# Decoder trunk, feed-forward: the last pair of chunks takes column blocks 2 and 3 by seven products instead of eight

## The reference

```python
def conv_glu_ffn(x, w_in, conv_w, conv_b, w_out):
    h = x @ w_in                                  # 2048 -> 2 x 5632
    hc = conv_b + sum(hp[:, k:k + S] * conv_w[k] for k in range(3))
    gate, val = jnp.split(hc, 2, axis=-1)
    return (gelu(gate) * val) @ w_out             # 5632 -> 2048

x = layer_norm(alpha * x + conv_glu_ffn(x, ...), gain, bias)
```

## Time and profile before

| | |
|---|---|
| median of three runs | 2014.38 us |
| the profiled execution | 2014.52 us |
| its span, first to last instruction | 2012.7 us |
| TensorE busy | 2003.1 us (100%), 10708 matmuls |
| weight loads busy | 1715.5 us (85%) |
| VectorE busy | 1657.6 us (82%), 1529 instructions |
| ScalarE busy | 1221.7 us (61%) |
| HBM read | 386.36 MB, 193 GB/s |

### The profile page before, as it was taken

The page is one execution under the profiler, slowest core; times in us unless marked ns, Lnnn a source line. Parts: engine busy times, 40 slices in busy tenths (PEclk is TensorE's granted clock), DMA queues, the critical chain, the costliest instruction groups (busy, mean ns, idle before and its releaser), DMA issues.

```text
span 2012.7 us, 25848 instructions
## 1 busy us (share of the span) xinstructions
PE 2003.1 (100%) x10708; PEld 1715.5 (85%) x10708; DVE 1657.6 (82%) x1529; ACT 1221.7 (61%) x1439; POOL 5.8 (0%) x10
## 2 busy tenths in 40 slices
PE   9999999999999999999999999999999999999998
PEld 8888888888888888888888877888888888888886
DVE  5446566769899998999997786776989899898998
ACT  5443444767566675766744664476766667576672
POOL 0000000000000000000000000000000000000001
PEclk9999999999999999999999999999999999999999
DMA  9554464655656565556656345465565656655662
GB/s 331 196 189 151 162 232 166 204 190 194 212 183 204 194 208 197 193 197 208 219 204 196 126 133 188 161 209 188 197 213 176 209 193 205 203 192 194 207 225 109
DMA packets 194824, 390.40 MB, mean 194 GB/s; under 512 B 6969, under 2 KB 9747, under 8 KB 193683
## 3 DMA queue, kind: packets, MB, share of 16 engines
q1 hardware_dynamic: 194419, 388.49, 57.6%
q10 hardware_dynamic: 288, 0.26, 0.1%
HBM read 386.36 MB, written 2.10 MB: 193 GB/s over the span
## 4 chain that ended last, share of the span: by engine, by line
PE 98%; DVE 1%; DMA 0%; SPq 0%; issue 0%; ACT 0%; DVEq 0%
PE ps L1550 37%; PE ps L1560 19%; PE ps L1879 6%; PE ps L1881 6%; PE ps L1880 6%; PE ps L1577 6%; PE ps L1579 5%; PE ps L1578 5%; PE ps L1700 1%; PE ps L2029 1%; PE ps L2004 1%; PE ps L2012 1%; PE ps L1667 0%; PE ps L1705 0%; PE ps L1538 0%; PE ps L1817 0%
## 5 line engine op out<-in xcount | busy, mean ns | idle before, releaser
L925 DVE TENSOR_TENSOR w_lo<-raw,w_hi 128x2048 fp32r<-128x2048 f32 x352 | 796.8, 2282 | 75.2 <-ACT w_hi L566 74.8
L566 ACT ACTIVATE w_hi<-raw 128x2048 fp32r<-128x2048 f32 x352 | 664.3, 1909 | 284.1 <-DMA raw<-ffn_w_in 116.6
L1550 PE MATMUL ps<-T,w_hi 128*128 128x512 f32 x3264 | 764.6, 390 | 0.0
L1550 PEld LDWEIGHTS ps<-T,w_hi 128*128 128x128 f32 x3264 | 605.7, 188 | 122.9 <-issue 1.7
L1560 PEld LDWEIGHTS ps<-T,w_lo 128*128 128x128 f32 x3264 | 405.8, 191 | 10.0 <-issue 2.0
L1560 PE MATMUL ps<-T,w_lo 128*128 128x256 f32 x3264 | 410.6, 283 | 0.0
L1879 PE MATMUL ps<-w_hi,forms 128*128 128x512 f32 x464 | 180.5, 389 | 0.0
L1881 PE MATMUL ps<-w_hi,forms 128*128 128x512 f32 x464 | 180.5, 389 | 0.0
L1577 PE MATMUL ps<-w_hi,T 128*128 128x512 f32 (+1 forms) x448 | 177.4, 396 | 0.1
L1579 PE MATMUL ps<-w_hi,T 128*128 128x512 f32 (+1 forms) x448 | 173.9, 388 | 0.0
L1578 PE MATMUL ps<-w_lo,T 128*128 128x512 f32 (+1 forms) x448 | 173.6, 388 | 0.0
(11 more groups left out here) (188 smaller groups left out, 1849.7 us busy)
## 6 DMA issues: line engine op xcount, KB each, us to landing
raw<-ffn_w_in SPq DMA_DIRECT2D x176, 1024.0 KB, 5.1
raw<-ffn_w_out SPq DMA_DIRECT2D x88, 1024.0 KB, 5.1
raw<-even_w_in SPq DMA_DIRECT2D x38, 1024.0 KB, 5.1
raw<-attn_w_qkv SPq DMA_DIRECT2D x20, 1024.0 KB, 5.2
raw<-even_w_out SPq DMA_DIRECT2D x16, 1024.0 KB, 5.1
raw<-attn_w_out SPq DMA_DIRECT2D x16, 1024.0 KB, 5.2
arena<-ln_gain SPq DMA_DIRECT2D x4, 1024.0 KB, 4.9
arena<-ln_bias SPq DMA_DIRECT2D x4, 1024.0 KB, 7.4
```

Source lines behind the costliest of these rows:

```text
L566: nc.scalar.activation(w_hi[:, s % RING], raw_at(s), ACT.Copy).then_inc(hi_ready, 1)
L925: vec.tensor_tensor(lo_at(s), raw_at(s), w_hi[:, s % RING].bitcast(F32), ALU.subtract).then_inc(lo_ready, 1)
L1550: ins = mm(ps[:, banks[j]], w_hi[:, s % RING, k, P * j:P * j + P], T[:, GK * kg + k], start=kg == 0 and k == 0, stop=kg == KG - 1 and k == ...
```

## The change

C of the last pair becomes a quad like the others, in both layers. On TensorE seven products of 12 matmuls stand where four blocks of 24 stood. The form X_21 is not made any more. VectorE makes four sums, seven low parts and nine takes for C where it made four low parts and two adds. The sums of this one quad (`LATE`) don't lie in `lnp`, since the gain and bias are loaded there by then, but in the second half of T (`late_sums`, with their low parts `late_lo` at the same place). Three of them are made in the middle of Q (`between`), the fourth in the quad as elsewhere; the tail's gated low parts are made in the middle of C. The tail's first block waits for C's takes (`quad_read`) instead of for the two adds.

```diff
-    place(C_AT, duo, PRODUCTS if duo < DUOS - 1 else KG)
+    place(C_AT, duo, PRODUCTS)
...
+LATE = [4 * k for k, (l, p, n) in enumerate(QUADS) if p == DUOS - 1 and n == 1]
...
+        with nc.sbuf_tensor("front_rows", [P, KT // 2, 2 * SEQ], F32R):
+            with nc.sbuf_tensor("late_sums", [P, 2, GK, COLS], F32) as late_sums:
+                pass
+            with nc.sbuf_tensor("late_lo", [P, 2, GK, COLS], F32R) as late_lo:
+                pass
...
 (ACT)
-                for j in range(KG + 2):
+                for j in range(PRODUCTS + 2):
                     high(s + j + HI_LEAD)
-                    if j in (1, 2):
-                        gated_high(j - 1)
-                    if j == 3:
+                    if j in (2, 3):
+                        gated_high(j - 2)
+                    if j == PRODUCTS - 1:
                         scale_gain(2 * l + 1)
...
 (VectorE)
+                def late_weight_sums():
+                    first_weight_sum(base + C_AT[DUOS - 1])
+                    weight_sums(base + C_AT[DUOS - 1])
...
-                def quad(s, x):
+                def quad(s, x, between=None):
...
                     take_product(s, x + 3, 1, 1, -1.0, 1)
                     low(s + 3 + LO_LEAD)
+                    if between is not None:
+                        between()
                     dve.wait_ge(used, s + 4)
                     take_product(s, x, 0, 1, -1.0)
...
-                    quad(base + Q_AT[p], 0)
+                    quad(base + Q_AT[p], 0, late_weight_sums if b == FC else None)
...
-                for j in range(KG):
-                    if j < 2:
-                        value_pair(c, j)
-                    low(s + j + LO_LEAD)
-                    if j == 1:
-                        gated_low(0)
-                    if j == 2:
-                        gated_low(1)
-                        dve.wait_ge(used, s + 2)
-                        add_chunk(2, 4, ffn_added)
-                dve.wait_ge(used, tail)
-                add_chunk(3, 6, ffn_added)
+                value_pair(c, 0)
+                value_pair(c, 1)
+                quad(base + C_AT[DUOS - 1], 4, gated_lows)
                 low(tail + LO_LEAD)
...
                 dve.wait_ge(used, s1 - ENDS)
+                dve.wait_ge(quad_read, READS * (QUAD_AT.index(base + C_AT[DUOS - 1]) + 1))
                 add_chunk(0, last_bank(0), ffn_added, out0 + 1)
...
 (TensorE)
-                        pair_output(p, 4, evicted(a, 1))
+                        quad(base + C_AT[p], 4, p, evicted(a, 1))
...
-                pe.wait_ge(ffn_added, outs + 1)
+                r = READS * (QUAD_AT.index(base + C_AT[DUOS - 1]) + 1)
+                pe.wait_ge(quad_read, r - 2)
...
-                pe.wait_ge(ffn_added, outs + 2)
+                pe.wait_ge(quad_read, r)
```

More of the change, by code:

```diff
@@ L107 @@
 SUM_COUNTS = {SUM_12: 1, SUM_24: 2, SUM_124: 3, SUM_ALL: 4}
-QUADS = [(l, p, n) for l in range(2) for p in range(DUOS) for n in ((0, 1) if p < DUOS - 1 else (0,))]
+QUADS = [(l, p, n) for l in range(2) for p in range(DUOS) for n in range(2)]
 QUAD_AT = [S_FFN[l] + (Q_AT[p] if n == 0 else C_AT[p]) for l, p, n in QUADS]
 SUMS = {s + i: (i, 4 * k + n) for k, s in enumerate(QUAD_AT) for i, n in SUM_COUNTS.items()}
+LATE = [4 * k for k, (l, p, n) in enumerate(QUADS) if p == DUOS - 1 and n == 1]
 SLOT_OF = [s for s in range(S_END) if s not in SUMS or SUMS[s][0] == SUM_24]
@@ L116 @@
 X_11, X_21, D_3, X_12, X_22, D_1, D_2, D_4 = range(FORMS)
-FORM_ENDS = [FORMS * l + (FORMS - 1) * ((DUOS - 1) * l + p) for l in range(2) for p in range(DUOS)] + [2 * (FORMS - 1) * (DUOS - 1) + 2 * FORMS]
+FORM_ENDS = [(FORMS - 1) * i for i in range(2 * DUOS + 1)]
 FORM_AT = {X_12: 0, X_22: 1, D_1: 2, D_2: 3, D_3: 4, D_4: 5}
@@ L357, in build_trunk, with is_late @@
         tokens = lambda n: half[:, n % 2].rearrange("p t n -> p (t n)")
+        def is_late(s):
+            i, count = SUMS[s]
+            return count - SUM_COUNTS[i] in LATE
         def raw_at(s):
@@ L362, in raw_at @@
                 return raw[:, LOAD_OF[s] % RING]
-            return lnp[:, SUM_PLACES[SUMS[s][0]]].rearrange("p (k n) -> p k n", k=GK)
+            place = SUM_PLACES[SUMS[s][0]]
+            if is_late(s):
+                return late_sums[:, place]
+            return lnp[:, place].rearrange("p (k n) -> p k n", k=GK)
         def lo_at(s):
-            return w_lo[:, LOAD_OF[s] % RING] if s in LOAD_OF else sum_lo[:, SUM_PLACES[SUMS[s][0]]]
+            if s in LOAD_OF:
+                return w_lo[:, LOAD_OF[s] % RING]
+            return (late_lo if is_late(s) else sum_lo)[:, SUM_PLACES[SUMS[s][0]]]
         def landed(s):
@@ L387, in forms_of @@
         def forms_of(p):
-            return [f for f in range(FORMS) if f != X_21 or p == DUOS - 1]
+            return [f for f in range(FORMS) if f != X_21]
         def form_count(l, p, f):
@@ L395, in ffn_counts @@
         def ffn_counts(l):
-            return S_FFN[l], TP_FFN[l], (2 + NCH) * l
+            return S_FFN[l], TP_FFN[l], NCH * l
         @block.sync
@@ L451, in ffn @@
                         chunk(b + 2)
[L452 to L455, removed]
+                    quad_blocks(p, 1, base + C_AT[p])
                 for n in range(NCH):
@@ L1269, in take_product, with gated_lows @@
                                              ALU.mult, ALU.add).then_inc(quad_read, 1)
+                def late_weight_sums():
+                    first_weight_sum(base + C_AT[DUOS - 1])
+                    weight_sums(base + C_AT[DUOS - 1])
+                def gated_lows():
+                    gated_low(0)
+                    gated_low(1)
                 def gate_and_sums(s, c, bank, q):
@@ L1359, in feed_forward @@
                 tail, c = base + TAIL_AT, FC - 1
-                s = base + C_AT[DUOS - 1]
-                for j in range(KG):
-                    if j < 2:
-                        value_pair(c, j)
-                    low(s + j + LO_LEAD)
-                    if j == 1:
-                        gated_low(0)
-                    if j == 2:
-                        gated_low(1)
-                        dve.wait_ge(used, s + 2)
-                        add_chunk(2, 4, ffn_added)
-                dve.wait_ge(used, tail)
-                add_chunk(3, 6, ffn_added)
+                value_pair(c, 0)
+                value_pair(c, 1)
+                quad(base + C_AT[DUOS - 1], 4, gated_lows)
                 low(tail + LO_LEAD)
-                m, out0, s1 = 2 * l + 1, outs + 2, tail + NCH
+                m, out0, s1 = 2 * l + 1, outs, tail + NCH
                 def last_piece_added(i):
@@ L1931, in quad @@
                     form_product(s + SUM_ALL, X_22, x + 3, False, more=True).then_inc(used, 1)
[L1933 to L1942, removed]
                 hidden(V_AT[0], 4, gate=True)
@@ L1975, in feed_forward @@
                     last_block(ends[-1][0])
-                    last_rows(outs + 2)
+                    last_rows(outs)
             feed_forward(0)
```

## The result

The changed kernel takes 2044.42 us (median of four runs, 2043.8 to 2045.37) against 2014.21 before on the same chips: ratio 1.015, 95% interval 1.0138 to 1.0162. It is slower by 30.2 us; 2044.5 was forecast.

A forecast was written before the change was run, and what follows sets the result against it. VectorE, full from Q to the tail with a 2.5 us lead, was taken to decide: 13.7 us lost in each of two layers plus 2.7 in the first layer's norm, 30.1 us, giving 2044.5 us, range 2036 to 2053.

The forecast's parts named there:

- The bound: From Q to the tail: VectorE is full, and TensorE sets the time only while VectorE delivers in time.
- lead of 2.5 us: At the tail's start before the change: VectorE's add into xres ends at 1978.00, TensorE starts the tail at 1980.49.
- TensorE's saving: Pair output C as a quad: twelve matmuls fewer, 2.72 us a layer, 5.44 for both layers.
- The walk down the queue: VectorE's work in order from Q's start: low(C+0) over at 24.25, tail at 54.5 instead of 40.80, 13.7 lost a layer.
- The stalls: TensorE's waits for VectorE ahead of C+0, C+1, C+3, C+4 and the tail: 5.2, 2.5, 3.7, 2.3, 2.7 us.
- Behind the tail: First layer's norm: fourth add 3.6 us late, less 0.9 cover, 2.7 us lost (0 to 3.6); second layer nothing.
- The sum: Whole kernel: 2 x 13.7 + 2.7 = 30.1 us more; span 2042.8, execution 2044.6, median 2044.5 us.
- Covers: ACT's added high parts and late taps (cover 2 us) and SP's loads for the sums: no cost while covered.
- Rival (b): TensorE's clock falls to half pace after the new stalls: 2057 us, or 2068 if the tail pays too; chance 0.08.
- a sign that it would be wrong: In the profile after: TensorE's granted clock falls; named among the things that would show the forecast wrong.
- Rival (a): TensorE is the bound throughout and its saving shows: 5.44 us less, 2008.9 us; chance 0.04.
- (c): Smaller loss, 2020 to 2036 us: VectorE has spare time the trace hides, or the tail is released earlier; chance 0.06.

The follow-up runs named there:

- e1: Changed kernel with the four late sums and their three high and low parts made for 64 of 512 columns only (incomplete): 2023.81 us, ratio 1.0046.
- e2: Changed kernel with the four late sums and ACT's high parts of three cut to 64 of 512 columns, low parts full size (incomplete): 2031.23 us.
- e5: Kernel before the change, with only the four sums' work added on VectorE (8.8 us a layer, read by nobody): 2030.13 us, ratio 1.0078.
- e3: Changed kernel, whole computation, with the two value pairs moved behind C's first take instead of ahead of its first low part: 2045.14 us.
- e4: Changed kernel, whole computation, with 22 more matmuls filling TensorE's first stall in each layer: 2044.27 us, ratio 1.0147.
- e7: e1 with 14 more matmuls in its one large stall, ahead of C+3, to keep TensorE busy (incomplete): 2020.46 us, ratio 1.0027.
- e6: Changed kernel with the late sums on GpSimd, ACT's first taps ahead of high(C+2), value pairs behind C's first take: 2059.48 us, ratio 1.0223.

## Why the prediction was right, point by point

- **The bound.** TensorE at 98% of the chain was no proof that its work decides; the second engine, full in the same stretch, with a lead of 2.5 us, was. e1, e2 and e5 show this: work taken off VectorE or laid on it moves the time with the number of TensorE's products unchanged.
- **TensorE's saving** of 2.72 us a layer is there (24 matmuls fewer), and inside the stalls. It can't be seen in any time.
- **The walk down the queue.** low(C+0) was forecast at 24.25 and came at 24.3; the tail at 54.5 and came at 54.6. The loss of a layer, 13.7, is 13.8. The stalls were forecast as 5.2, 2.5, 3.7, 2.3 and 2.7. They are 5.32, 0.22, 3.43, 0.42 and 2.31 in the first layer: the second and the fourth are small because the products ahead of them ran at half pace. TensorE's idle time is 11.7 us and not 16; the difference went into slow matmuls.
- **Behind the tail.** 2.7 us were forecast in the first layer's norm. From the first layer's Q to the second's it is 971.42 us (1955.93 - 984.51) against 955.32 (1939.69 - 984.37), 16.10 more; less 13.78 that is 2.3. The wait ahead of the first turned piece is only 0.48; eight matmuls near the tail's start had run at about half pace, which made TensorE 1.6 us later and hid the rest. In e3 and e4, where the clock held in the tail, that wait is 2.08, and the piece starts 20.72 us after the tail in all three (18.36 before). The 2.7 was mis-sized by little: the fourth add came 17.1 us after the tail's start and not 17.4, and the cover is 1.0 us by the rows (1043.53 - 1042.53), where 0.9 was taken. In the second layer nothing was to be added, and the fourth add starts 13.89 after the tail instead of 13.80.
- **The sum.** 0.1 + 13.8 + 2.3 + 13.8 = 30.0, and the last stretch, from the tail on, is 0.7 shorter (31.48 against 32.21; not in VectorE's part, which is 14.06 and 14.07 from the fourth add to its last instruction, but in what follows it). The span is 29.3 us longer, 30.1 were forecast. It need not be the change's: the stretch is 31.4 in e5 too, whose tail is that of the kernel before, and the executions of that kernel have spans from 2012.0 to 2013.1 us.
- **The last digit is luck.** The changed kernel's four executions lie in two groups, 2043.8 twice and 2045.0 and 2045.4. The traced one is of the lower group, 0.8 us under the 2044.6 forecast for it; the median of 2044.42 lies between the groups, and its distance of 0.1 us from the forecast says nothing of the working's accuracy.
- **Covers.** ACT's late taps and the loads ended no wait of TensorE, as forecast.
- **Rival (b), the clock.** Half of it happened: the granted clock fell to 0.50 after the first stall in both layers, and fell again later. The prediction had named this as a sign that it would be wrong, and there it was too strict: up to the tail the fall cost nothing, since VectorE was late behind it (e4). The Trainium skill's rule that I weighed (TensorE: Matmul & The Clock Gate, HAM oscillation: gaps bring the clock to its half level) agrees with the trace of the first stall, at 0.50 for 1980.40 to 1985.70, but not with "each time": after idle times of 2.18 and 2.31 us in e4 no matmul was slow. The price depends on who is waited for next: nothing up to the tail in the changed kernel, 1.6 to 2.7 us after a stall where TensorE decides again (e5, e7).
- **Where the clock does cost in the whole computation.** Behind the wait ahead of the first turned piece TensorE has no idle time and decides again. These are the piece in e3, the six us from it on there, and the same six us in the changed kernel's trace:

```profile
1059.90 0.66 PE L1684 MATMUL ps<-ident,xres 128*128 128x128 f32 x4 [2.08 <-DVE xres L1001]
1059.90:1065.90 6.00, 6.00 (x24) 4.90 (x25) 5.02 (x8) 1.20 (x2) 0.00 (x0) 0.72 0.04 16
1059.80:1065.80 6.00, 5.99 (x33) 5.04 (x34) 5.89 (x9) 2.17 (x4) 0.00 (x0) 1.00 0.44 160
```

  From the piece to the second layer's Q it is 896.12 us in the changed kernel (1955.93 - 1059.81) and 897.37 in e3, with a granted clock of 0.72 instead of 1.00 in these six us: 1.2 us lost, which no term of the prediction has. The profiles of e2, e4 and e7 show the same fall there, those of e1 and e6 don't, with about the same wait of 2.0 to 2.1 us in all of them. It fits the distance between the two groups of the changed kernel's executions and e3's 0.7 us, and it takes back a part of e7's gain; as only one execution of each kernel has a trace, that is not shown.
- **Rival (a)**, TensorE as the bound, and **(c)**, spare time that the trace hides, are ruled out by the result itself and by e1, e2 and e5.

What stays open: the 0.5 us of e7, the 0.7 us in the last stretch, and what makes the clock fall behind a wait of 2 us in one execution and not in another. No version of this quad beats the kernel before in any run. With the late sums and their low parts cut to an eighth (e1, e7) it is still 2020 to 2024 us; by the queue that is because nine takes stand where two adds stood and the value pairs stand ahead of C+3, where the one large stall is. Another place for the sums' work that reads no second SBUF operand was not tried.

## What to carry to other kernels

A change that takes matmuls away and gives an engine beside it element-wise work must be paid from the lead that this engine has at that place, not from its average share: here 82% over the program, 100% in the stretch, and 2.5 us of lead against 17.9 of new work. Write that engine's queue down instruction by instruction with start-to-start times from the trace; that gave the distance to 0.1 us where this engine is late to the end of the stretch (the changed kernel, e3, e4) and to 0.2 in e2. It was 1 to 3 us low where TensorE decides again behind a stall and its clock has fallen (e1, e5), and 16 us low where two engines held each other up (e6). Don't count stalls as costs: moving one (e3) or filling one (e4) changed nothing, and the sum of the work did.

## What the runs showed of the hardware

- A pass of VectorE and one of GpSimd, each with two SBUF operands, took turns: in e6 VectorE's 2.28 us became 6.03 to 6.71, each ending 2.14 to 2.16 us after GpSimd's pass that it met. VectorE's pass with one operand from PSUM wasn't held up (0.68).
- GpSimd's add over 128x2048 took 6.15 to 6.5 us against VectorE's passes and 4.84 once in the second layer; each ended 4.4 to 4.5 us after VectorE's pass that it met.
- After stalls of 5.3 and 5.8 us some 6 to 12 of TensorE's next matmuls of 512 columns started 0.43 us apart instead of 0.227 (the changed kernel, e3, e5). After shorter ones the length of the stall alone didn't tell: after 3.3 to 3.6 us mostly from the first to the seventh matmul on, but in one stall of 3.5 (e6, first layer) not at all; after 1.9 and 2.1 us in e2 for 7 to 8 of them, and after 2.2 and 2.3 us in e4 for none.
